# Feed-forward tails: one VectorE operation moved ahead of another, and sums of adaptive weights with 128 columns

## The reference

```python
for i in range(DEPTH_2):                      # 4 layers, x is 256 x 1024, float32
    mod = einsum('bd,sde->sbe', cond, ada_w[i]) + ada_b[i]      # 2 sites x 3072
    shift, scale, gate = split(mod, 3)
    h = x * (1 + scale[0]) + shift[0]
    y = mixer_i(h, ...)
    x = layer_norm(ALPHA * x + (1 + gate[0]) * y, ln_g[i, 0], ln_b[i, 0])
    h = x * (1 + scale[1]) + shift[1]
    y = swiglu(h, ffn_w_in[i], ffn_w_out[i])  # 1024 -> 2 x 2816 -> 1024
    x = layer_norm(ALPHA * x + (1 + gate[1]) * y, ln_g[i, 1], ln_b[i, 1])
```

## Time and profile before

| | |
|---|---|
| median of 3 runs | 2367.32 us (2365.84 to 2368.16) |
| the profiled execution | 2368.6 us, its span 2366.8 us |
| TensorE busy | 2259.0 us, 95% |
| TensorE weight loads busy | 1908.5 us, 81% |
| VectorE busy | 1801.2 us, 76% |
| ScalarE busy | 1160.2 us, 49% |
| mean granted clock of TensorE | 0.974 of full speed |

### The profile page before, as it was taken

The page is one execution under the profiler, slowest core; times in us unless marked ns, Lnnn a source line. Parts: engine busy times, 40 slices in busy tenths (PEclk is TensorE's granted clock), DMA queues, the critical chain, the costliest instruction groups (busy, mean ns, idle before and its releaser), DMA issues. The chain is left out here.

```text
span 2366.8 us, 30136 instructions
## 1 busy us (share of the span) xinstructions
PE 2259.0 (95%) x11857; PEld 1908.5 (81%) x11857; DVE 1801.2 (76%) x2133; ACT 1160.2 (49%) x1213; POOL 137.6 (6%) x237
## 2 busy tenths in 40 slices
PE   7999988999999999989999999999998999998997
PEld 7888667888888888878788887888987887897886
DVE  6887577598888888856888677886796887777555
ACT  4443244577767677645433364343653434464432
POOL 2000100000000000000011000110001111000000
PEclk9999998899999999999999899999999999899999
DMA  8844553399999999954699535995633998344552
GB/s 303 260 131 150 174 162 106 130 370 367 362 362 366 356 369 358 366 173 143 208 373 349 173 125 174 372 350 189 187 130 121 316 354 296 123 143 154 188 191 71
DMA packets 346767, 567.80 MB, mean 240 GB/s; under 512 B 69248, under 2 KB 182400, under 8 KB 346624
## 3 DMA queue, kind: packets, MB, share of 16 engines
q1 hardware_dynamic: 325632, 490.31, 61.0%
q0 software_dynamic: 20992, 75.54, 8.6%
HBM read 564.71 MB, written 1.05 MB: 239 GB/s over the span
## 5 line engine op out<-in xcount | busy, mean ns | idle before, releaser
L285 DVE TENSOR_TENSOR st_lo<-st_raw,st_hi 128x2048 fp32r<-128x2048 f32 (+1 forms) x195 | 440.7, 2266 | 107.9 <-ACT st_hi L275 107.7
L285 DVE TENSOR_TENSOR es_lo<-es_raw,es_hi 128x2048 fp32r<-128x2048 f32 x192 | 429.4, 2285 | 73.3 <-ACT es_hi L275 72.8
L313 PE MATMUL ps<-st_hi,sb_h_hi 128*128 128x512 f32 (+1 forms) x1232 | 462.7, 376 | 15.3 <-DVE sb_h_lo L1167 6.2
L275 ACT CAST st_hi<-st_raw 128x2048 fp32r<-128x2048 f32 (+1 forms) x195 | 368.3, 1893 | 212.5 <-PE ps L315 181.8
L315 PE MATMUL ps<-st_hi,sb_h_lo 128*128 128x512 f32 (+1 forms) x1232 | 452.5, 367 | 0.0
L314 PE MATMUL ps<-st_lo,sb_h_hi 128*128 128x512 f32 (+1 forms) x1232 | 451.8, 367 | 0.0
L275 ACT CAST es_hi<-es_raw 128x2048 fp32r<-128x2048 f32 x192 | 357.0, 1909 | 46.4 <-PE ps L315 27.0
L313 PEld LDWEIGHTS ps<-st_hi,sb_h_hi 128*128 128x128 f32 x1232 | 233.7, 190 | 57.9 <-issue 12.3
L315 PEld LDWEIGHTS ps<-st_hi,sb_h_lo 128*128 128x128 f32 x1232 | 233.1, 189 | 38.6
L314 PEld LDWEIGHTS ps<-st_lo,sb_h_hi 128*128 128x128 f32 x1232 | 233.7, 190 | 36.0 <-issue 0.5
L313 PE MATMUL ps<-es_hi,moe_hg_hi 128*128 128x512 f32 x512 | 204.4, 399 | 0.8 <-PEq L61 0.8
(11 more groups left out here) (704 smaller groups left out, 3806.2 us busy)
## 6 DMA issues: line engine op xcount, KB each, us to landing
st_raw<-in_ffn_w_in_dram SPq DMA_DIRECT2D x176, 512.0 KB, 5.8
t_aw<-in_ada_w_dram POOLq DMA_DIRECT2D x144, 512.0 KB, 6.5
es_raw<-in_w_expert_gate_dram SPq DMA_DIRECT2D x64, 1024.0 KB, 8.0
es_raw<-in_w_expert_up_dram SPq DMA_DIRECT2D x64, 1024.0 KB, 7.3
es_raw<-in_w_expert_down_dram SPq DMA_DIRECT2D x64, 1024.0 KB, 7.1
st_raw<-in_ffn_w_out_dram SPq DMA_DIRECT2D x44, 1024.0 KB, 7.3
fb_aw<-in_ada_w_dram SPq DMA_DIRECT2D x39, 512.0 KB, 6.1
hs_raw<-in_w_in_dram SPq DMA_DIRECT2D x36, 512.0 KB, 6.9
```

The lines of the kernel that those rows point to most:

```text
L275: act.copy(p.at(self.hi[:, m % self.held, :]), p.at(self.raw[:, n % self.slots, :])).then_inc(self.high, 1)
L285: dve.tensor_tensor(p.at(self.lo[:, m % self.held, :]), p.at(self.raw[:, n % self.slots, :]), p.at(self.hi[:, m % self.held, :]).bitcast(F ...
L313: pe.matmul(out, a_hi, b_hi, start=start, stop=False, skip_group_check=True)
```

## The change

Two edits, both in `layer_tail`. On VectorE, the loop over the blocks no longer reaches piece `f_end`; that piece is split after the last block's rows. In `column_sums` each matmul streams all 128 columns of the matrix of ones (`k.ones[:]`) in place of one, and writes 128 equal columns from column `i` on. The next matmul writes over all of them but the first, so that columns 0 to 15 hold the same sums as before; columns 16 to 142 of the bank are written too.

```diff
@@ column_sums(s, bank)
                 for i in range(16):
-                    op = pe.matmul(ps[:, bank, i:i + 1], ada[:, s, i * P:(i + 1) * P], k.ones[:, 0:1], start=True, stop=True)
+                    op = pe.matmul(ps[:, bank, i:i + P], ada[:, s, i * P:(i + 1) * P], k.ones[:], start=True, stop=True)
@@ VectorE's program
             for n, (kind, b, a) in enumerate(order):
-                S.lower(dve, min(f0 + n + S.held, f_end + 1))
+                S.lower(dve, min(f0 + n + S.held, f_end))
@@
             split_hidden(N_BLOCKS - 1)
+            S.lower(dve, f_end + 1)
```

## The result

| | before | after |
|---|---|---|
| median of 5 runs | 2367.32 us (2359.56 to 2368.16) | 2348.65 us (2347.33 to 2349.86) |
| ratio, 95% interval | | 0.9928 (0.9912 to 0.9944) |
| the profiled execution | 2368.6 us, span 2366.8 us | 2347.33 us, span 2345.6 us |
| mean granted clock of TensorE | 0.974 | 0.981 |

The change makes the kernel 18.7 us faster by the medians, 0.79%; the ratio in the table puts it at 0.72%. The forecast was 2349.4 us.

A forecast was written before the change was run, and what follows sets the result against it. TensorE bounds the ends of tails 0 to 2, losing time to a wait and two slow-clock stretches. 4.9 + 0 + 11.2 + 1.8 = 17.9 us gives a median of 2349.4 us; own range 2347 to 2352, eight in ten 2346 to 2355.5.

The forecast's parts named there:

- The wait: TensorE's 1.64 us standstill for the rows' remainder in tails 0 to 2 goes with VectorE's new order: 4.9 us.
- The pass: Sums' passes with 128 columns hide under the weight loads, still 0.118 us each: cost 0, at most 25 us.
- The higher price: By the skill's issue-gap ratio a 128-column pass would be nearer 0.16 than 0.118 us, costing some 8 us.
- The clock over the products: From the wait's end through the tails' products, the clock stays at 1.00 instead of 0.70 to 0.78: 11.2 us gained.
- Its cause: The products' clock falls after a wait between one-column matmuls; the last tail's 1.40 us wait alone did not lower it.
- The second stretch: 16 transposes after the second sums at full clock: ScalarE starts after 1.40 us, not 1.88, 2.12, 2.00; 1.8 us gained.
- The slow second stretch: Rival: transposes stay slow, 2351.2 us, or a slow stretch moves into the next stage, 2354.5 us; chance 0.17.

The follow-up runs named there:

- e2: Kernel before with only the sums widened to 128 columns, VectorE's order kept; 2353.22 us, ratio 0.9945.
- e7: Kernel before, old order, with 15 of the first site's 16 one-column sums left out; 2350.12 us, one run, beside 2372.1 us of before.
- e1: Changed kernel with one-column sums again, so only VectorE's order differs from the kernel before; 2351.38 us, ratio 0.9939.
- e10: Changed kernel with one-column sums, order alone, run once more on another chip; 2358.55 us beside 2372.1 us of before.
- e5: Changed kernel, but the first site's sums, woven between products, keep one column and the second site's are wide; 2352.21 us, ratio 0.9932.
- e3: Changed kernel, but the second site's 16 sums, behind the last product, keep one column; 2350.84 us, ratio 0.9935.

## Why the prediction was right

The forecast missed the median by 0.75 us. That close a hit is partly luck: the changed kernel's runs reach from 2342.52 to 2351.44 us over its four series, with medians of 2346.26 to 2348.65. What the tails show is sharper. By the forecast's terms:

- **The wait: right.** 4.9 us predicted. First products start 2.17 us after the first load instead of 3.90, 1.72 us a tail and 5.2 us in all (2.18 and 3.90 in the others); e2, which keeps the wait, has 5.2 us more in its tails (61.4 - 56.2). The idle time of the matmuls on which the term was built is a little shorter than the delay.
- **The pass: right.** 0 predicted, 0 measured: 3.77 us for 32 passes, 0.118 us each; between products, three products with eight passes take 1.59 us (1621.12 to 1622.71 in tail 1) where the prediction had 1.58 from before. The higher price from the Trainium skill's "TensorE: Matmul & The Clock Gate", section "Back-to-back issue gap", an estimate of 0.16 us, did not appear in these passes; by the page's ratio of 81 to 56 ns the estimate is 0.17 us, and the extra cost 10 us rather than 8.
- **The clock over the products: right in size.** 11.2 us predicted. From the first product to the second sums it took 16.04, 14.45 and 14.45 us before (19.94 - 3.90 and so on) and takes 11.25, 11.25 and 11.23 us now: 4.8 + 3.2 + 3.2 = 11.2 us. The clock is 1.00 in the 27 products' parts of nine profiles with first sums of 128 columns, whether the wait is there (e2) or not.
- **Its cause: right in the main, too narrow in one sentence.** The prediction read the fall as a wait between one-column matmuls. Either edit takes most of it: 14.5 us for the order alone, 12.7 us for the columns alone, 18.4 us for both, by medians of one series. The two don't add up, since both act on the same fall. But "a wait alone did not lower the clock there" holds for the 1.40 us of the earlier trace rows and the 1.53 us of e2, and not for the 2.42 us of e7. And one-column passes without a wait do it in 4 of 9 tails (e1, e10, e5). How much the order alone is worth is not sharp: 14.5 us by e1's median, 9.8 us by the tails of its profile (73.9 - 64.1), whose execution took 2355.91 us, 4.5 more than that median; the runs of this one program reach from 2349.94 to 2358.55 us. Whether the wait makes a fall more certain is not shown either: 3 tails of 3 with it, 4 of 9 without.
- **The second stretch: right in kind, mis-sized.** 1.8 us predicted, 0.33 + 0.58 + 0.45 = 1.36 measured. ScalarE starts 1.55 us after the first transpose's load, not 1.40, because TensorE waits in the middle for the normed rows. In tail 1:

```profile
1636.13 0.86 PEld L934 LDWEIGHTS ps<-ident,X 128*128 128x128 f32 x8
...
1637.13 0.87 PEld L934 LDWEIGHTS ps<-ident,X 128*128 128x128 f32 x8 [0.15 <-DVE X L1153]
...
1637.67 2.84 ACT L1086 ACTIVATE t_full<-ps,cols 128x256 f32<-128x256 f32 x6 [4.30 <-PE ps L934]
```

  The price of 1.40 us came from a place whose last operand was ready 0.54 us before the first load (VectorE's step there ended at 2163.44, the load began at 2163.98); here VectorE is still making the second half while TensorE turns the first. With TensorE faster, VectorE is the next limit at this point.
- **The rivals.** The slow second stretch did not stay. e3 shows it was a near thing: it needs the second site wide. The rule of the Trainium skill, "TensorE: Matmul & The Clock Gate", section "Part 4: PE-mode transpose", that transposes do not count as busy in the same way, is neither needed nor refuted here: behind wide sums 16 transposes passed at 1.00, behind one-column sums they ran slow in 13 of 15 tails (before, e1, e3, e7, e10). What came before them went with it: the transposes are the same in all these runs.
- **What was not foreseen.** The two profiled executions differ by 21.2 us of span, 3.5 more than their tails; the first load of tail 0 is 6.3 us earlier although nothing ahead of it was changed. The forecast took the profile for an average execution of before, which it was to 1.3 us; the profile of after was 1.3 us under its median. The spread of the runs lies outside the tails: the four profiles of the changed kernel have spans from 2340.7 to 2349.5 us and tails of 56.2 to 56.3. Over the four series the change gains 18.7, 18.4, 19.8 and 20.4 us, each more than the tails' 17.7; where the rest comes from is open, if it is more than spread.

The terms as measured are 5.2 + 0 + 11.2 + 1.4 = 17.8 us, the tails taken whole give 17.7, and the medians differ by 18.7 us; the 1.0 us between is less than the runs' spread. The wait came out 0.3 us larger than forecast and the second stretch 0.4 us smaller, and the two nearly cancel.

## What to carry to other kernels

Read the granted clock beside the busy share, and where it falls, look at what TensorE did before: a wait, or matmuls that load full weights and stream one column. Here such sums stream 128 columns in the time of one, if the PSUM columns behind them are free; no width between 1 and 128 was run, so it is not known from how many columns on the clock stays up. When two edits work on one fall of the clock, price them together, and repeat a profile before a difference in the clock is put down to an edit.

## What the runs showed of the hardware

- A plain float32 pass with one column and one with 128 columns follow each other at the same 0.118 us, so it is not the columns that set it.
- One-column passes lowered the clock from full speed with TensorE never waiting: in 32 passes and the 16 transposes behind them it fell to 0.50 (e1, e3). The same with 128 columns kept 1.00 in 27 of 27 tails of nine profiles.
- A wait of 2.42 us lowered it in 3 of 3 tails (e7), one of 1.53 us between wide sums in 0 of 3 (e2), one of 1.4 us with no sums beside it in 0 of 14 (the last tail of every profile), and one of 1.64 us between one-column passes came ahead of a fall in 3 of 3 (before).
- The same program with the same instructions fell in tail 2's products in one execution and not in the other (e1, e10), which is worth 3.2 us. The spread of the runs alone does not show such falls: the changed kernel, whose tails fell in none of four profiles, has runs from 2342.52 to 2351.44 us, as far apart as those of this program (2349.94 to 2358.55 us).
